# Two transformer layers and a third block on one core: the last down product of each feed-forward part interleaved with the start of the next stage

## What is computed

```
for l in range(2):
    h = rms_norm(x, norm1_g[l]);  z = h @ w_in[l]          # first use of x in a layer
    ...mLSTM, sparse attention and retention branches, gated...
    x = x + y @ w_out
    h2 = rms_norm(x, norm2_g[l])
    x = x + (silu(h2 @ w_gate) * (h2 @ w_up)) @ w_down     # d_ff 2816
x = rms_norm(x, final_norm_g)
h = rms_norm(x, mix_norm_g_2);  proj = h @ w_in_2          # second block
...attention, state space mixer, 16 experts...
```

## Time and profile before

| | |
|---|---|
| timed runs, median of 3 | 1767.31 us (1765.33 to 1767.56) |
| profiled execution | 1773.4 us, its span 1771.4 us |
| TensorE busy | 1639.5 us, 93% |
| GpSimd busy | 1423.5 us, 80% |
| ACT, DVE busy | 796.6 us (45%), 711.6 us (40%) |
| mean granted TensorE clock | 0.961 of full |
| chain that ended last | GpSimd 54%, TensorE 23%, issue 20% |
| last down product of the feed-forward part ends | 517 us (layer 0), 1026 us (layer 1) |

### The profile page before, as it was taken

The page is one execution under the profiler, slowest core; times in us unless marked ns, Lnnn a source line. Parts: engine busy times, 40 slices in busy tenths (PEclk is TensorE's granted clock), DMA queues, the critical chain, the costliest instruction groups (busy, mean ns, idle before and its releaser), DMA issues.

```text
span 1771.4 us, 24042 instructions
## 1 busy us (share of the span) xinstructions
PE 1639.5 (93%) x7218; PEld 1267.2 (72%) x7218; DVE 711.6 (40%) x1363; ACT 796.6 (45%) x982; POOL 1423.5 (80%) x1579
## 2 busy tenths in 40 slices
PE   7899999999989798999999978899899999999976
PEld 5667777788867677777788767678675887666654
DVE  3595754201027667733100059175445221222225
ACT  4534444444434344534444435345323444555542
POOL 6778798799977796878999958777564778999992
PEclk9989999999989799999999989998999999999997
DMA  5543344555544343445555544655255767999980
GB/s 205 189 144 130 119 155 140 173 188 178 185 148 143 119 139 107 136 138 166 186 188 178 182 142 140 245 189 198 94 209 216 258 221 276 385 380 384 385 297 25
DMA packets 94056, 340.01 MB, mean 192 GB/s; under 512 B 10272, under 2 KB 14896, under 8 KB 93520
## 3 DMA queue, kind: packets, MB, share of 16 engines
q1 hardware_dynamic: 90656, 318.79, 52.0%
q10 hardware_dynamic: 2160, 15.90, 2.5%
q0 software_dynamic: 1152, 4.19, 0.7%
HBM read 326.24 MB, written 25.19 MB: 198 GB/s over the span
## 4 chain that ended last, share of the span: by engine, by line
POOL 54%; PE 23%; issue 20%; DMA 1%; DVE 1%; POOLq 1%; ACT 0%; DVEq 0%; SPq 0%; ACTq 0%
POOL w_lo L1507 52%; PE bank L1011 7%; PE bank L1039 6%; PE bank L1008 5%; PE bank L535 3%; POOL w_lo L1514 1%; PE bank L1054 1%; DVE x L2192 0%; DMA rows_by_expert<-gates,tiny 0%; POOLq L1502 0%; PE bank L1025 0%; DMA gates<-rows_by_expert 0%; PE bank L966 0%; DMA raw<-outputs_by_expert,tiny 0%; PE bank L564 0%
## 5 line engine op out<-in xcount | busy, mean ns | idle before, releaser
L1507 POOL TENSOR_TENSOR w_lo<-raw,w_hi 128x256 fp32r<-128x256 f32 x1416 | 1063.3, 788 | 243.2 <-ACT w_hi L1146 242.1
L535 PE MATMUL bank<-w_hi,hT 128*128 128x512 f32 x2240 | 742.8, 414 | 60.4 <-POOL w_lo L1507 29.5
L1146 ACT ACTIVATE w_hi<-raw 128x1024 fp32r<-128x1024 f32 x356 | 376.5, 1058 | 588.1 <-PE bank L535 411.0
L535 PEld LDWEIGHTS bank<-w_hi,hT 128*128 128x128 f32 x2240 | 429.5, 196 | 174.6 <-POOL w_lo L1507 35.5
L535 PE MATMUL bank<-w_lo,hT 128*128 128x512 f32 x1120 | 455.9, 407 | 0.0
L1514 POOL TENSOR_TENSOR w_lo<-arena,w_hi 128x1024 fp32r<-128x1024 f32 x146 | 345.4, 2393 | 58.7 <-ACT w_hi L1146 58.5
L535 PEld LDWEIGHTS bank<-w_lo,hT 128*128 128x128 f32 x1120 | 219.0, 196 | 54.3
L1146 ACT ACTIVATE w_hi<-arena 128x1024 fp32r<-128x1024 f32 x146 | 154.3, 1058 | 115.7 <-PE bank L1011 58.8
L832 PE MATMUL bank<-w_hi,mixT 128*128 128x512 f32 x352 | 110.8, 396 | 4.0 <-DVE mixT L1895 4.0
L1039 PE MATMUL bank<-w_hi,mixT 128*128 128x512 f32 x320 | 107.3, 416 | 0.2 <-POOL w_lo L1514 0.2
L535 PE MATMUL bank<-w_hi,mixT 128*128 128x512 f32 x304 | 98.2, 404 | 7.7 <-DVE xn L1861 2.0
(11 more groups left out here) (354 smaller groups left out, 1931.6 us busy)
## 6 DMA issues: line engine op xcount, KB each, us to landing
raw<-in_stream SPq DMA_DIRECT2D x356, 512.0 KB, 3.3
arena<-in_experts SPq DMA_DIRECT2D x192, 512.0 KB, 6.4
rows_by_expert<-in_blank ACTq DMA_DIRECT2D x18, 512.0 KB, 5.2
gates<-rows_by_expert SPq DMA_DIRECT2D x12, 512.0 KB, 5.7
outputs_by_expert<-xn SPq DMA_DIRECT2D x12, 512.0 KB, 5.6
arena<-in_stream SPq DMA_DIRECT2D x10, 512.0 KB, 6.1
gates<-rows_by_expert SPq DMA_DIRECT2D x3, 1024.0 KB, 4.9
outputs_by_expert<-xn SPq DMA_DIRECT2D x3, 1024.0 KB, 5.1
```

Of the source, the lines that this page charges most:

```text
L535: mm = pe.matmul(LIN[t][:, :], lhs[:, a, k0 + k, t * P:(t + 1) * P], w[:, k, :], start=(k0 + k == 0 and n == 0), stop=(k0 + k == nk - 1 an ...
L1146: act.activation(w_hi[:, s, :], src, ACT.Copy).then_inc(s_hi, 1)
L1507: part = nc.gpsimd.tensor_tensor(w_lo[:, i, c], raw[:, i, c], w_hi[:, i, c].bitcast(F32), ALU.subtract)
```

## The change

- The loop of the feed-forward part runs nine times. The last two groups are written out: hidden, group, then a down product in whose middle (between n = 0 and n = 1) the last hidden group is turned (`halfway=hidden`), and then the last down product, which reads its own tile `heT_last`.
- In the last down product DVE adds each bank to x when its token tile is done (a new semaphore `s_first` for token tile 0), and TensorE turns the first four column tiles of x between the two token tiles of n = 1 (`between=x_first_half`). ACT and DVE split these four inside the same stretch; DVE puts its last addition behind the split.
- The next stage therefore starts with `fed=True`. Before the first layer the same turning and splitting stands ahead of the layer loop.
- The small parameters of every layer get eight more columns (ones, or `final_norm_g` for the second block), by which DVE multiplies the gain in `next_gain`, in every layer, during the last feed-forward groups.

The diff, cut; the changes to the host's tables and to the declarations (`N1_FACTOR`, `SMALL_END`, `S_END`, `s_first`, the new count `first`) are left out:

```diff
@@ -229,6 +229,7 @@
         onehot_sb = arena[0:BUCKETS, 1024:1024 + 2 * WIN].rearrange("p (t w) -> p t w", t=2)
+        heT_last = mixT[:, 1].rearrange("p a k t -> p (a k t)")[:, 0:2 * QK * SEQ].rearrange("p (a k t) -> p a k t", a=2, k=QK)
         cqT = mixT[:, 2].rearrange("p a k t -> p (a k t)")[:, 0:2 * QK * SEQ].rearrange("p (a k t) -> p a k t", a=2, k=QK)
@@ -585,8 +587,7 @@
-                pe.wait_ge(s_x, xr.up())
-                product(hT, KT, "act", feed=(x_cols, lambda: pe.wait_ge(s_x, xr.up())))
+                product(hT, KT, "act", feed=(x_cols, lambda: pe.wait_ge(s_x, xr.up())), fed=True)
                 product(hT, KT, "act")
@@ -736,12 +737,19 @@
                 seed()
-                with repeat(pe, "ff_pe", FF_GROUPS - 1, counts, per):
+                with repeat(pe, "ff_pe", FF_GROUPS - 2, counts, per):
                     hidden()
                     group()
                     down()
                 hidden()
-                down()
+                free.clear()
+                group()
+                down(halfway=hidden)
+                down(heT_last, between=x_first_half)
+
+            def x_first_half():
+                pe.wait_ge(s_x, xr.up())
+                transposed(x_cols, KT // 2)
 
@@ -821,16 +829,22 @@
-            def down():
+            def down(hidden_t=heT, halfway=None, between=None):
 
                 pe.wait_ge(s_td, tr.back(0))
                 for n in range(2):
+                    if halfway and n:
+                        halfway()
                     hi, lw = quarter()
                     for t in range(TT):
+                        if between and (n, t) == (1, 1):
+                            between()
                         for k in range(QK):
                             for a, w in ((0, hi), (1, hi), (0, lw)):
-                                mm = pe.matmul(AB[2 * t + n][:, :], heT[:, a, k, t * P:(t + 1) * P], w[:, k, :],
+                                mm = pe.matmul(AB[2 * t + n][:, :], hidden_t[:, a, k, t * P:(t + 1) * P], w[:, k, :],
                                                start=False, stop=True, skip_group_check=True)
+                        if between and t == 0:
+                            mm.then_inc(s_first, 1)
                     mm.then_inc(s_used, 1)
@@ -1110,6 +1123,7 @@
             pe.wait_ge(s_cst, 32)
+            x_first_half()
             with repeat(pe, "layers_pe", LAYERS, counts, per) as l:
@@ -1217,8 +1231,7 @@
             def layer(l):
-                act.wait_ge(s_sm, smc.up(32))
-                unit(4, lambda t: copy(sm[:, t, :], t), early=x_root, feed=(hT, L_N1))
+                unit(4, lambda t: copy(sm[:, t, :], t), early=x_root, feed=(hT, L_N1), fed=True)
                 unit(4, lambda t: copy(mqk_tok[:, t, :], t))
@@ -1298,28 +1311,34 @@
-            def hidden_high():
+            def hidden_high(dst=heT):
                 act.wait_ge(s_tr, tr.up())
-                act.activation(heT[:, 0].rearrange("p k t -> p (k t)"), TR[(tr.n - 1) % 2][:, :], ACT.Copy).then_inc(s_th, 1)
+                act.activation(dst[:, 0].rearrange("p k t -> p (k t)"), TR[(tr.n - 1) % 2][:, :], ACT.Copy).then_inc(s_th, 1)
 
             def feed_forward(name, groups, l):
                 glu(first=x_root, feed=L_N2)
 
                 act.dma_start(small[:], small_in[l + 1]).then_inc(s_sm, 16)
                 act.dma_start(gain1, gains[0]).then_inc(s_sm, 16)
-                with repeat(act, name, groups - 1, counts, per):
+                with repeat(act, name, groups - 2, counts, per):
                     hidden_high()
                     glu()
                     high()
                     high()
                     pos.up(2)
                 hidden_high()
+                glu()
+                hidden_high(heT_last)
                 high()
                 high()
                 pos.up(2)
+                high()
+                act.wait_ge(s_arg, arg.up())
+                split(hT, KT // 2, L_N1)
+                high()
+                pos.up(2)
 
             def second():
-                act.wait_ge(s_sm, smc.up(32))
                 act.dma_start(bflat, alibi).then_inc(s_alibi, 16)
@@ -1327,8 +1346,7 @@
-                act.activation(sw[:, 0, :], small[:, S_SW:S_G1], ACT.Copy).then_inc(s_sw, 1)
-                act.wait_ge(s_arg, arg.up())
+                act.activation(sw[:, 0, :], small[:, S_SW:S_END], ACT.Copy).then_inc(s_sw, 1)
 
@@ -1343,7 +1361,7 @@
-                unit(4, by_token(0), early=lambda: roots(2), first=x_root, feed=(hT, S_N1))
+                unit(4, by_token(0), early=lambda: roots(2), first=x_root, feed=(hT, S_N1), fed=True)
                 unit(4, by_token(1), mid=dt_logs)
@@ -1488,6 +1506,8 @@
                 high()
+            act.wait_ge(s_sm, smc.up(32))
+            split(hT, KT // 2, L_N1)
             with repeat(act, "layers_act", LAYERS, counts, per) as l:
@@ -1586,13 +1606,12 @@
-            def x_stats(gain, then=None):
-
-                split(hT, KT // 2, gain)
+            def x_stats(gain, fed=False):
+
+                if not fed:
+                    split(hT, KT // 2, gain)
                 x_squares()
                 split(hT, KT // 2, gain, KT // 2)
-                if then:
-                    then()
                 rstd(2, X_INV).then_inc(s_rs, 1)
@@ -1888,35 +1907,46 @@
-            def hidden_low():
+            def hidden_low(dst=heT):
                 dve.wait_ge(s_th, th.up())
                 tr.up()
                 b = TR[(tr.n - 1) % 2]
-                dve.tensor_tensor(heT[:, 1].rearrange("p k t -> p (k t)"), b[:, :],
-                                  heT[:, 0].rearrange("p k t -> p (k t)").bitcast(F32), ALU.subtract).then_inc(s_td, 1)
+                dve.tensor_tensor(dst[:, 1].rearrange("p k t -> p (k t)"), b[:, :],
+                                  dst[:, 0].rearrange("p k t -> p (k t)").bitcast(F32), ALU.subtract).then_inc(s_td, 1)
 
             def x_back():
 
                 for n in range(2):
-                    for t in range(TT):
-                        v = x[:, t, n * 512:(n + 1) * 512]
-                        i = dve.tensor_tensor(v, AB[2 * t + n][:, :], v, ALU.add)
-                    i.then_inc(s_x, 1)
+                    dve.wait_ge(s_first, first.up())
+                    v = x[:, 0, n * 512:(n + 1) * 512]
+                    dve.tensor_tensor(v, AB[n][:, :], v, ALU.add)
+                    if n:
+                        split(hT, KT // 2, L_N1)
+                    dve.wait_ge(s_used, pos.up())
+                    v = x[:, 1, n * 512:(n + 1) * 512]
+                    dve.tensor_tensor(v, AB[2 + n][:, :], v, ALU.add).then_inc(s_x, 1)
                 dve.wait_ge(s_x, xr.up(2))
+
+            def next_gain():
+                dve.wait_ge(s_sm, smc.up(32))
+                g = small[:, L_N1:L_N1 + KT]
+                dve.tensor_tensor(g, g, small[:, N1_FACTOR:N1_FACTOR + KT], ALU.mult).then_inc(s_arg, 1)
 
             def feed_forward(name, groups):
                 glu()
-                with repeat(dve, name, groups - 1, counts, per):
+                with repeat(dve, name, groups - 2, counts, per):
                     hidden_low()
                     glu()
                     pos.up(2)
                 hidden_low()
-                dve.wait_ge(s_used, pos.up(2))
+                glu()
+                pos.up(2)
+                next_gain()
+                hidden_low(heT_last)
                 x_back()
 
             def layer(l):
-                dve.wait_ge(s_sm, smc.up(32))
-                x_stats(L_N1)
+                x_stats(L_N1, fed=True)
                 small_norms()
@@ -2196,13 +2226,9 @@
             def second():
-                dve.wait_ge(s_sm, smc.up(32))
-                g = small[:, S_N1:S_N1 + KT]
-                dve.tensor_tensor(g, g, small[:, S_G1:S_G1 + KT], ALU.mult).then_inc(s_arg, 1)
                 dve.memset(conv2[:, :, 0:3], 0.0)
-                split(hT, KT // 2, S_N1)
                 dve.wait_ge(s_sw, 1)
-                dve.tensor_tensor(sw[:, 1, :], small[:, S_SW:S_G1], sw[:, 0, :].bitcast(F32), ALU.subtract).then_inc(s_nx, 1)
+                dve.tensor_tensor(sw[:, 1, :], small[:, S_SW:S_END], sw[:, 0, :].bitcast(F32), ALU.subtract).then_inc(s_nx, 1)
                 x_squares()
```

24 lines of the change are left out of this document (13 added, 11 removed).

## The result

| | before | after |
|---|---|---|
| timed runs, median of 4 | 1767.43 us (1765.33 to 1770.5) | 1739.72 us (1732.66 to 1744.39) |
| ratio, 95% interval | | 0.9833 [0.9815, 0.9852] |
| profiled execution, its span | 1773.4, 1771.4 us | 1737.69, 1735.6 us |

What follows compares the result with a forecast made beforehand. The steady feed-forward loop was taken as bound by TensorE, GpSimd just behind, the ends by other engines' chains. Gains of 8.8 + 7.8 + 1.3 = 17.9 us off 1767.31 gave 1749.4 us, range 1744 to 1758.

Steps and rivals of the forecast that it cites:

- (f): Eight more columns in one load, one semaphore, one unrolled feed-forward iteration: -0.3 to +0.5 us, taken as 0.
- (a): Last hidden group turned between halves of the down product before: gap of 2.00 us gone at each layer's end.
- (b): x added and turned by halves inside the last down product: no gap; next layer could begin at 3.9, before 10.2.
- (c): Layer 0 to 1, with loop jumps: fifth quarter 18.8 us after e, the last half product's start; gain 6.8 us.
- The rival of the clock: Clock falls in both transitions, one quarter each at 5.1 instead of 2.8: 4.7 us lost, 1754; chance 0.08.
- (d): Layer 1 to second block, no jump: scaled matmul at e + 24.1, before 29.9; gain 5.8 us.
- (e): Start: first half split ahead of the loop, table load moved behind it; first product earlier, gain 1.3 us.
- GpSimd as the bound: New DVE work slows GpSimd; TensorE starves 2 to 3 us at each end; gain 12 to 14 us; chance 0.12.
- the sign named for this rival: GpSimd parts of 0.8 us and over through the end, with TensorE waiting for them.
- the contention between DVE and GpSimd: Two-input DVE and SBUF-reading GpSimd instructions block each other whole; named within the GpSimd rival, without its own chance.

Runs made afterwards that it cites:

- the other kernel with equal offsets: Kernel before with an unused 32-byte tile ahead of everything and `small` 32 bytes wider, so weights and `hT`, `mixT` start 32 past a multiple of 64: 0.9914.
- the padded kernel: Kernel before with the tile `small` 8 unused columns wider, so all tiles behind it lie 32 bytes further: ratio 0.9939.
- the shifted one: Changed kernel with tiles at 32 past a multiple of 64, plus four tiny DVE memsets ahead of the held operation: 0.9903, 17.2 us gain.
- the one with its tiles put back: Changed kernel with `small` 8 columns wider still, so tiles behind it lie 32 bytes past a multiple of 64 as before: 0.993, 12.4 us gain.
- the second profile: Changed kernel, unchanged, run again beside the written-out one: 0.983 against the kernel before, 1742.16 us.

## Why the prediction was wrong in size

**The step that failed is (f).** "Eight more columns in one load" was taken at 0, with bounds of -0.3 to +0.5 us, because no row gave it a price. Its price was a gain of 10.8 us (0.9939; 6 to 16 by the interval), and 15.2 (0.9914) in the other kernel with equal offsets. I had looked at it as a load and as operations, and not as an allocation that moves every tile behind it. With the padded kernel as the base, the changed one is 0.9833 / 0.9939 = 0.9893, 19 us; the other way about, with the misaligned layout on both sides, it is 12.4 us in one kernel and 17.2 in the shifted one, whose medians are the same (above). The 17.9 us of the interleaving lie between 12.4 and 19, and no measurement here fixes them better than to some 4 us.

**(a)** held for the most part: 2.00 us gone at each end, 4.0 forecast, 3.2 and 3.8 in the whole change by the leads; alone only 1.6, because of the multiplication of the gain. Nothing is late behind it (the rounding of 0.60 us at 499.00 on ACT delays one w_hi).

**(b)** held: additions of 0.69 us, no wait for x inside the product, and 3.86 us from e to the first quarter where no jump stands in between.

**(c)** held in its mechanism. TensorE's branch took 3.53 us in the profile after, 4.19 in the second one (3.64 was taken), and DVE was away from 509.5 to 513.5, 4.0 us (3.4 was taken). Line 168, start in us of the branch and of the first instruction behind it:

```profile
L168 PEldq COMPARE_BRANCH  x1: 3531/3531/3531, 505.4 to 505.4; - x1
...
L168 PEldq FUSED_REGOPS  x1: 50/50/50, 509.0 to 509.0; - x1
...
L168 DVEq COMPARE_BRANCH  x1: 63/63/63, 509.5 to 509.5; - x1
...
L168 DVEq MOVE  x1: 43/43/43, 513.5 to 513.5; - x1
```

The fifth quarter, put at e + 18.8, came at 19.5 with full clock and at 20.6 with the fall; over the whole end, 8.8 us had been forecast, and the lead rose by 8.7 with full clock, 7.9 with the fall. In the old layout, where none of it can be the layout's, it rose by 8.8 with full clock (the shifted kernel) and by 6.9 with a fall (the one with its tiles put back). **The rival of the clock** came true in the profiled execution and not in its repetition at this end: four groups of three from 517.72 to 522.04, 4.3 us for a quarter of 2.7. It had been priced for both transitions at 4.7 us; here it cost 1.6 at the first end and 1.7 at the second (4.45 us from 1016.88 to 1021.33), part of it in time that TensorE would have waited.

**(d)** 25.1 instead of 24.1; 7.3 us instead of 7.8 in this profile and 7.0 in three others. The step that was wrong is that ACT would have the fourth pair ready: DVE ended it at e + 15.2, not 14.3, after the wait of 0.89 us shown above (1.24 in the second profile). Ahead of that rounding ACT had waited 3.69 us for a load of weights that SP issued at 1006.65 and that landed at 1014.03, 7.4 us, where the load before took 3.1. The two loads that ACT issues at the head of the second block, at 1005.60 and 1005.96, were under way beside it; that they made it slow wasn't tested. In the kernel before this load took 6.5 us too, but nobody waited for it. The rest of the chain took 9.2 us instead of 8.9. The gap ahead of the scaled matmul was 2.5 us and not 3.9 only where TensorE had done the fourth quarter at half clock; in three other profiles it was 3.96, 4.48 and 4.54.

**(e)** held: the table load went from 13.2 to 14.49, into the loop's first w_hi, and the first product starts 1.43 us earlier (1.3 forecast). By the Trainium skill (ScalarE: Activation LUTs, What ACT_TABLE_LOAD costs) with its drain for each switch it would have been 2.7, an estimate; the trace speaks against the drain here, since the load starts 0.02 us after the activation ahead of it ends (12.92 + 1.55).

**GpSimd as the bound** (0.12) did not come: in the steady loop it still waits for ACT, and its 12 parts beside the new DVE work of layer 0's end took 8.37 us, 0.70 each. At the second end it had 16 parts in 16.21 us, 1.01 each: eleven of 0.7 to 0.95 and five of 1.7 beside the squares and the gain products. That is the sign named for this rival, but without its consequence: the waits of TensorE there ended with DVE and ACT. What I had named as a mere tail of this rival, the contention between DVE and GpSimd, showed itself elsewhere and the other way about: single DVE operations were held, in the change's kernels and in the kernel before alike (5.11 us at 129.4 for one of 0.36). The Trainium skill (SBUF - State Buffer, Who interferes with whom) lets a two-input DVE operation and a GpSimd instruction block each other until the first is through. The rows at 546.67 agree in direction, but 8.41 us is the length of twelve GpSimd instructions, and not of one.

**What stays open.** The measured gain (29.5 us by the ratio) is about 10.8 + 17.9 = 28.7, so no large part is unexplained, but each term is known to 3 or 4 us at best, since held operations move single executions by that much. What decides whether one is held, beyond the moment, was not found. Why the distance of the two starts sets TensorE's step was not shown, only that it does.

## What to carry to other kernels

Before a declaration grows by a few columns, work out where every tile behind it will start, and look at the step between matmuls before and after; a kernel bound by TensorE can gain or lose half a per cent by 32 bytes, and that is easily taken for the effect of the change itself. An unused tile of the same size in the old kernel separates the two. Where the first product after a loop's jump is wanted at once, try the loop written out: four microseconds of jump are hidden only as long as something else is waiting anyway. Here the medians gave 4.8 us for it across two chips and 4.4 us on one chip, with intervals that overlap. And when a chain is moved forward, look for what doesn't move with it: here a load of weights, late in both kernels, came onto the path.

## What the hardware showed that was not expected

- Matmuls of 128x512 at full clock, with a weight load for each, step in 0.227 us (0.68 for three) when the two operands' starts lie a multiple of 256 bytes apart, and in 0.233 us (0.70) when they lie 32 bytes off that. The Trainium skill (SBUF - State Buffer, Who interferes with whom) gives TensorE two independent read ports, one for each operand, and says that it waits for no one; a step that depends on both places at once speaks against full independence.
- A DVE operation on 128x6 values, else 0.17 to 0.73 us, took 8.41, 11.30 and 11.62 us in three profiles beside a GpSimd that ran on, and each time ended within 0.03 us of the end of the part behind which GpSimd paused, for 0.03 us or more.
- The jump to the head of a loop cost 3.5 to 4.2 us on TensorE's queue, 3.4 to 4.4 on DVE's and 2.7 to 3.3 on ACT's (508.2 to 511.5 in the profile after).
- Of two executions of one kernel, the clock fell to half its level behind gaps of 1.13 and 1.90 us in one and stayed full behind 1.87 and 1.59 in the other. In two further kernels with the same end it fell behind 1.11 and 2.36 us and stayed full behind 1.55 and 1.54; in the kernel before it stayed full behind a single gap of 2.00.
